# Output projection in products of 512 columns, its rows and weights in another order, and the last job's blocks added one by one

## The reference, cut to what matters

```
merged = sum over four branches of sigmoid(gate_i) * (y_i @ P_i)
x  = x + merged @ W_o                       # W_o: 1024 x 1024
h2 = rmsnorm(x) * norm2_g
x  = x + square(relu(h2 @ W_up)) @ W_down   # W_up: 1024 x 4096, W_down: 4096 x 1024
return x                                    # 512 x 1024
```

## Time and profile before

| | us |
|---|---|
| median of three runs | 1216.63 |
| lowest, highest | 1214.82, 1216.95 |
| the profiled execution's own time | 1213.98 |
| its span in the trace | 1212.2 |
| TensorE busy in the span | 1180.3 |
| DVE, ACT, POOL busy | 504.2, 489.4, 468.8 |

### The profile page before, as it was taken

The page is one execution under the profiler, slowest core; times in us unless marked ns, Lnnn a source line. Parts: engine busy times, 40 slices in busy tenths (PEclk is TensorE's granted clock), DMA queues, the critical chain, the costliest instruction groups (busy, mean ns, idle before and its releaser), DMA issues.

```text
span 1212.2 us, 21083 instructions
## 1 busy us (share of the span) xinstructions
PE 1180.3 (97%) x8974; PEld 973.9 (80%) x8974; DVE 504.2 (42%) x1001; ACT 489.4 (40%) x808; POOL 468.8 (39%) x288
## 2 busy tenths in 40 slices
PE   8999999999999899999999999999899999999998
PEld 7998877887788588667777777789888888888886
DVE  4799435455554544443453676361522000222000
ACT  6455323232223444775726534423543312344220
POOL 3443435325442234323323622433344544344541
PEclk9999999999999999999999999999999999999999
DMA  6222323222221142212522312323122323232330
GB/s 248 88 73 84 115 80 111 69 70 93 98 78 54 35 147 81 64 35 68 193 74 77 104 41 70 138 89 105 53 95 97 122 93 98 71 103 97 112 122 35
DMA packets 35855, 111.49 MB, mean 92 GB/s; under 512 B 4257, under 2 KB 8865, under 8 KB 35250
## 3 DMA queue, kind: packets, MB, share of 16 engines
q1 hardware_dynamic: 30144, 98.59, 24.6%
q10 hardware_dynamic: 5106, 11.43, 2.6%
q0 software_dynamic: 512, 0.13, 0.1%
HBM read 99.43 MB, written 9.04 MB: 89 GB/s over the span
## 4 chain that ended last, share of the span: by engine, by line
PE 81%; DVE 10%; ACT 5%; POOL 2%; issue 2%; DMA 0%; DVEq 0%; ACTq 0%
PE pst L1803 18%; PE pst L1805 17%; PE pst L1804 17%; PE pst L1992 5%; PE pst L1993 5%; PE pst L1994 5%; POOL w_lo L799 1%; PE pst L2314 1%; ACT w_hi L917 1%; PE pst L2306 1%; DVE x_lo L1663 1%; PE pst L2092 1%; PE pst L2039 1%; PE pst L2276 1%; PE pst L2291 1%
## 5 line engine op out<-in xcount | busy, mean ns | idle before, releaser
L799 POOL TENSOR_TENSOR w_lo<-raw,w_hi 128x1024 fp32r<-128x1024 f32 x164 | 402.6, 2461 | 642.4 <-ACT w_hi L917 630.7
L1803 PE MATMUL pst<-h_hi,w_hi 128*128 128x512 f32 (+1 forms) x704 | 255.9, 363 | 1.3 <-DVE h_lo L1369 0.7
L1805 PE MATMUL pst<-h_hi,w_lo 128*128 128x512 f32 (+1 forms) x704 | 243.2, 345 | 0.0
L1804 PE MATMUL pst<-h_lo,w_hi 128*128 128x512 f32 (+1 forms) x704 | 242.9, 345 | 0.0
L917 ACT ACTIVATE w_hi<-raw 128x1024 fp32r<-128x1024 f32 x164 | 171.3, 1051 | 147.7 <-PE pst L1994 114.2
L1803 PEld LDWEIGHTS pst<-h_hi,w_hi 128*128 128x128 f32 x704 | 133.4, 189 | 25.3 <-issue 4.7
L1805 PEld LDWEIGHTS pst<-h_hi,w_lo 128*128 128x128 f32 x704 | 133.3, 189 | 15.9
L1804 PEld LDWEIGHTS pst<-h_lo,w_hi 128*128 128x128 f32 x704 | 133.6, 190 | 15.1 <-issue 2.2
L1803 PE MATMUL pst<-x_hi,w_hi 128*128 128x512 f32 (+1 forms) x272 | 102.7, 377 | 3.8 <-POOL w_lo L799 2.0
L1805 PE MATMUL pst<-x_hi,w_lo 128*128 128x512 f32 (+1 forms) x272 | 102.4, 377 | 0.0
L1804 PE MATMUL pst<-x_lo,w_hi 128*128 128x512 f32 (+1 forms) x272 | 102.4, 376 | 0.0
(11 more groups left out here) (338 smaller groups left out, 2062.9 us busy)
## 6 DMA issues: line engine op xcount, KB each, us to landing
raw<-in_weights SPq DMA_DIRECT2D x164, 512.0 KB, 3.4
xt<-in_x SPq DMA_DIRECT2D x4, 512.0 KB, 5.4
wait_gate<-stage ACTq DMA_DIRECT2D x8, 256.0 KB, 2.7
gate_t<-wait_gate ACTq DMA_DIRECT2D x1, 2048.0 KB, 9.0
x<-in_x ACTq DMA_DIRECT2D x1, 2048.0 KB, 7.8
out<-x SPq DMA_DIRECT2D x8, 256.0 KB, 3.1
cst<-in_consts SPq DMA_DIRECT2D x1, 1524.0 KB, 11.1
wait_ret_g<-stage ACTq DMA_DIRECT2D x4, 256.0 KB, 3.0
```

What stands on the lines that cost most here:

```text
L799: nc.gpsimd.tensor_tensor(w_lo[:, u % W_SLOTS, :], raw[:, u % RAW_SLOTS, :], w_hi[:, u % W_SLOTS, :].bitcast(F32), ALU.subtract).then_inc( ...
L1803: M(out, lh, rh, start=(first and i == 0), stop=False)
L1804: M(out, lh, rl, start=False, stop=False)
L1805: last = M(out, ll, rh, start=False, stop=(final and i == len(terms) - 1))
```

## The change

1. W_o is cut into 2 halves of 512 columns in place of 4 quarters of 256, and a weight unit holds 256 rows by 512 columns of it. A matmul has 512 columns. PHASE_O has 8 jobs (half c, pair of tiles kk).
2. For c = 0, and for kk = 0 of c = 1, a job runs tiles 2kk and 2kk+1 over all four blocks. Each block has a PSUM bank of its own for each half (`wo_bank`). The rest of c = 1 is done block by block in `wo_rows(b)`: 6 tiles by 3 matmuls.
3. DVE adds half 0 in four instructions of 512 columns after job (0, 3), and half 1 of block b in `wo_rows(b)`. On DVE `norm2_low(b - 2)` now stands ahead of the addition of block b.
4. One unit's conversion (`jobs(1)`) stands inside the loop of blocks, and one behind `norm2_low(NB - 1)`, ahead of the up jobs.
5. In the last down job a block's last matmul counts `rows_done`; DVE adds blocks 0 to 2 one by one, and block 3 in two pieces of 256 columns, each with an output DMA of its own.

```diff
-PHASE_O = [("wo", c, b) for c in range(4) for b in range(NB)]
+PHASE_O = [("wo", c, kk) for c in range(2) for kk in range(KD // 2)]
...
     if kind == "wo":
-        return [("w_o", 2 * a), ("w_o", 2 * a + 1)]
+        return [("w_o", b, a)]
...
+            if kind == "wo":
+                return job_out["wo"], 4 * a + max(b - 1, 0)
...
+        def wo_bank(c, blk):
+            if c == 0:
+                return 4 + blk
+            s = job_slot(JOB_NO[("up", 0, 0)])
+            return [2 * s, 2 - 2 * s, 1, 3][blk]
...
-            jobs(len(PHASE_O) - NB - 1)
+            jobs(KD // 2 + 2)
             g("norm2_tables")
-            jobs(1)
             for b in range(NB):
-                jobs(1)
                 if b >= 2:
                     g("norm2_low", b - 2)
+                g("wo_rows", b)
+                if b == NB - 1:
+                    jobs(1)
                 g("norm2", b)
                 if b:
                     g("norm2_turn", b - 1)
...
             g("norm2_low", NB - 1)
+            jobs(1)
             for half in range(2):
...
+            def output(b, c0, c1, added):
+                sp.wait_ge(job_out["down"], added)
+                sp.dma_start(out[0, P * b:P * b + P, c0:c1], x2[:, b, c0:c1]).then_inc(out_done, 16)
+
             for c in range(2):
-                for b in range(NB):
-                    sp.wait_ge(job_out["down"], 8 + 4 * c + b + 1)
-                    sp.dma_start(out[0, P * b:P * b + P, T * c:T * c + T], x2[:, b, T * c:T * c + T])\
-                        .then_inc(out_done, 16)
-            sp.wait_ge(out_done, 16 * 2 * NB)
+                for b in range(NB - c):
+                    output(b, T * c, T * c + T, 8 + 4 * c + b + 1)
+            for i in range(2):
+                output(NB - 1, T + 2 * P * i, T + 2 * P * i + 2 * P, 16 + i)
+            sp.wait_ge(out_done, 16 * (2 * NB + 1))
...
-                act.wait_ge(*all_out("wo", ("wo", 3, b)))
+                act.wait_ge(job_out["wo"], NB + b + 1)
...
                 elif kind == "wo":
-                    dve.wait_ge(x2_in, 16)
-                    dst = x2[:, b, 2 * P * a:2 * P * a + 2 * P]
-                    V.tensor_tensor(dst, pst[:, 2 * s, 0:2 * P], dst, ALU.add).then_inc(job_out[kind], 1)
+                    if (a, b) == (0, KD // 2 - 1):
+                        dve.wait_ge(x2_in, 16)
+                        dve.wait_ge(dense_done, n + 1)
+                        for blk in range(NB):
+                            wo_add(0, blk)
...
+                    if n == len(JOBS) - 1:
+                        for blk in range(NB + 1):
+                            part = slice(T * c, T * c + T)
+                            if blk < NB - 1:
+                                dve.wait_ge(rows_done, NB - 1 + blk + 1)
+                            else:
+                                dve.wait_ge(dense_done, n + 1)
+                            if blk >= NB - 1:
+                                part = slice(T * c + 2 * P * (blk - NB + 1), T * c + 2 * P * (blk - NB + 2))
+                            dst = x2[:, min(blk, NB - 1), part]
+                            src = pst[:, down_bank(c, min(blk, NB - 1)), part.start - T * c:part.stop - T * c]
+                            V.tensor_tensor(dst, src, dst, ALU.add).then_inc(job_out["down"], 1)
...
+            def wo_rows(b):
+                if b < NB - 1:
+                    dve.wait_ge(rows_done, b + 1)
+                else:
+                    dve.wait_ge(dense_done, JOB_NO[PHASE_O[-1]] + 1)
+                wo_add(1, b)
...
+                    if a == 0 or b == 0:
+                        pe.wait_ge(lo_ready, u + 1)
+                        for k in (2 * b, 2 * b + 1):
+                            for blk in range(NB):
+                                if a == blk == 0:
+                                    pe.wait_ge(m_lo, k + 1)
+                                last = wo_part(a, k, blk)
                         last.then_inc(dense_done, 1)
...
+                            if n == len(JOBS) - 1 and j == 1 and blk < NB - 1:
+                                last.then_inc(rows_done, 1)
...
+            def wo_rows(b):
+                for k in range(2, KD):
+                    if b == 0 and k % 2 == 0:
+                        pe.wait_ge(lo_ready, UNIT_NO[("w_o", k // 2, 1)] + 1)
+                    last = wo_part(1, k, b)
+                    if b == NB - 1 and k % 2 == 1:
+                        last.then_inc(dense_done, 1)
+                if b < NB - 1:
+                    last.then_inc(rows_done, 1)
```

More of the change, by code:

```diff
@@ L145 @@
 SPILL_NO = {n: i for i, n in enumerate(n for n, j in enumerate(JOBS) if j[0] in SPILLED)}
-assert all(UNIT_NO[units_of(j)[0]] % 2 == 0 for j in JOBS if j[0] in ("av", "bv", "wo"))
+assert all(UNIT_NO[units_of(j)[0]] % 2 == 0 for j in JOBS if j[0] in ("av", "bv"))
 assert UNIT_NO[("w_in", BV + 2)] % W_SLOTS + 3 <= W_SLOTS
@@ L573, in build @@
         YSW_STEPS = NB
+        rows_done = sem("rows_done")
         br_order = [BRANCH_RW, BRANCH_SB, BRANCH_RET, BRANCH_SW]
@@ L1939, in job @@
                 elif kind == "wo":
-                    job_begin(n)
-                    us = u % W_SLOTS
-                    def wo_part(m, blk, k):
-                        toks = slice(P * blk, P * blk + P)
-                        return product3(pst[:, 2 * job_slot(m), 0:2 * P].rearrange("p (a f) -> p a f", a=2),
-                                        [((x_hi[:, k, toks], x_lo[:, k, toks]),
-                                          (w_hi[:, us:us + 2, P * k:P * k + P], w_lo[:, us:us + 2, P * k:P * k + P]))],
-                                        k == 0, k == KD - 1)
-                    if a == 0 and b < 2:
-                        for k in range(KD - 1):
-                            if b == 0:
-                                pe.wait_ge(m_lo, k + 1)
-                            wo_part(n, b, k)
-                        if b == 1:
-                            pe.wait_ge(m_lo, KD)
-                            wo_part(n - 1, 0, KD - 1).then_inc(dense_done, 1)
-                            wo_part(n, 1, KD - 1).then_inc(dense_done, 1)
-                    else:
-                        for k in range(KD):
-                            last = wo_part(n, b, k)
+                    if a == 0 or b == 0:
[5 more added lines that the diff above has]
+                                last = wo_part(a, k, blk)
                         last.then_inc(dense_done, 1)
@@ L1994, in job, with wo_part @@
                             last = M(o, u_lo[:, f, toks], w_hi[:, us, ws], start=False, stop=(f == FH - 1))
+                            if n == len(JOBS) - 1 and j == 1 and blk < NB - 1:
+                                last.then_inc(rows_done, 1)
                     last.then_inc(dense_done, 1)
+            def wo_part(c, k, blk):
+                u, at_ = UNIT_NO[("w_o", k // 2, c)] % W_SLOTS, T * (k % 2)
+                toks = slice(P * blk, P * blk + P)
+                return product3(pst[:, wo_bank(c, blk), :], [((x_hi[:, k, toks], x_lo[:, k, toks]),
+                                                             (w_hi[:, u, at_:at_ + T], w_lo[:, u, at_:at_ + T]))],
+                                k == 0, k == KD - 1)
+            def wo_rows(b):
[7 more added lines that the diff above has]
+                    last.then_inc(rows_done, 1)
             def sb_rows(h):
@@ L2418, in _ @@
                 ret_out=ret_out, ret_sum=ret_sum, sw_sum=sw_sum, sw_scores=sw_scores,
-                sw_turn=sw_turn, sw_out=sw_out, norm2_turn=norm2_turn, up_early=up_early))
+                sw_turn=sw_turn, sw_out=sw_out, wo_rows=wo_rows, norm2_turn=norm2_turn, up_early=up_early))
 def host_layout(inp):
```

15 lines of the change are left out of this document (9 added, 6 removed).

## The result

| | before | changed |
|---|---|---|
| median | 1215.72 (4 runs, 1214.32 to 1216.95) | 1203.45 (4 runs, 1203.16 to 1203.61) |
| the profiled execution's own time | 1213.98 | 1203.32 |
| its span | 1212.2 | 1201.6 |

The account below looks back on a forecast made before the run. The prediction took TensorE's queue, its waits and the tail behind its last matmul as the bound. A stage gain of 8.1 us and a tail gain of 1.7 made -9.8, giving 1206.8 us, range 1203.8 to 1210.0.

Parts of the forecast that it names:

- Wider products: Output projection: 192 matmuls of 512 columns replace 384 of 256, saving a fixed 0.014 us on each of 192: -2.7 us.
- The first wait: Start of the output projection: the first wo matmul no longer waits for DVE to empty a bank: -0.4 us.
- the short one: Output projection, at 808.81 us: a short wait for an emptied bank goes as well: -0.2 us.
- Weights of wo: Output projection: converted weight units arrive before TensorE wants them, with 4 us of slack: cost 0.
- The norm of each block: Behind the output projection: block 0's turn stops waiting, -1.0; `up_early(0)` waits 0.9 instead of 2.05, -1.2; block 3, +0.1 us.
- The third up unit: Ahead of the third up job: its weights, converted earlier, are ready at 858.7 and wanted at 861.3, removing a wait: -2.1 us.
- The stage as a whole: Output projection through norm: counted forward, the first full up job starts at 861.3 instead of 869.41: -8.1 us.
- The tail: Behind the last matmul: DVE adds blocks as they end and finishes at 1207.8 instead of 1209.49: -1.7 us.
- Total: Whole kernel: -9.8 us, own time 1204.2 for the profiled execution; against the median, 1216.63 - 9.8 = 1206.8.
- a median that lies 2.5 lower in its spread: Low end of the range: the changed kernel's median might lie 2.5 us lower, as the profiled execution does.
- 0.5 for the last DMA: End of the kernel: a smaller last output DMA with an empty queue could gain 0 to 0.5 us; taken as 0.
- the extra conversion on ACT and POOL: Norm stage: ACT's 1.0 us is covered with 0.9 to spare; POOL overlapping block 3's h2n would cost 0.7 at most.

Follow-up runs that it names:

- experiment 7: The changed kernel with each 512-column product of the output projection made of two of 256: 1206.38 us, beside 1204.15 for the changed kernel.
- experiment 2: The kernel before with only the last down job's blocks added as they end and block 3 in two pieces: 1213.05 us, beside 1215.65 unedited.
- experiment 8: The changed kernel, unedited, timed again: 1204.15 us (4 runs), ratio 0.9910 to the kernel before.
- experiment 4: The changed kernel with the third up weight unit converted behind the first up job again, as before: 1207.40 us (5 runs).
- experiment 6: The kernel before, unedited, traced in two more executions: 1215.65 and 1215.26 us.
- experiment 5: The kernel before with the third up weight unit converted early, behind the last wo job: 1211.57 us, beside 1214.92 unedited.
- experiment 11: The changed kernel with its last two down jobs run block by block, plus a gate-job piece between the first two sliding-window score jobs: 1203.57 us.

## Why the sum was right and the range was not

**What held, step by step.** *Wider products*, 2.7: 2.6 by experiment 7, at 0.2266 and 0.1200. *The first wait*, 0.4, and the short one: gone. *Weights of wo*, 0: no wait. *The norm of each block*: the turn of block 0 waits for nothing; ahead of `up_early(0)` 0.63 are left where I had 0.9, because ACT's copies of block 1 led to a low part that ended 846.83 + 1.27, a little sooner than by my steps; block 3 waits for nothing where I had 0.1. POOL's instruction (847.97 to 850.37) ended ahead of block 3's h2n at 850.39, which took 0.75: no collision, by 0.02 us. *The third up unit*: ready at 857.9 (855.51 + 2.40), wanted at 860.76. The stage as a whole: -8.26 for -8.1. *The tail*: -1.85 for -1.7, confirmed alone by experiment 2. Forecast for the profiled execution: own time 1204.2. It was 1203.32; of the 0.9 between them 0.4 lies ahead of all that was changed, 0.2 in the stage, 0.15 in the tail and 0.1 in up and down.

**The step that failed** is the last one, in *Total*: the profiled execution "was 2.65 below the median of the runs shown, which I take as the spread of executions", and all of that was carried over to the changed kernel. In the changed kernel the profiled execution was 0.13 below its median, not 2.65. The spread was no fixed offset that every version of the kernel keeps. The kernel before has two places where TensorE's clock falls to 1.2 GHz for 3.4 us in some executions: the scores, at 1.2 to 1.4 us a fall, and behind the wait for the third up unit, at 1.6 to 1.7. The profiled execution had neither: of 56 others only 10 had a mean clock of 0.999 or more (median 1213.6), and the median of all was 1215.8. Those at 0.996, 23 of them, have a median of 1216.37, 2.8 above 1213.6, and one fall of each kind is 2.8 to 3.1. The change removes the second place with its wait and leaves the first. So of the 12.3 us, about 10.2 are the difference without falls (1213.6 - 1203.45). The other 2.1 are the falls: in part those behind the wait, which can no longer come, and in part luck, since none of the changed kernel's first four executions had the fall in the scores, which it still has in some (10.8 in place of 12.3 by experiment 8).

That the wait brings falls is shown by the traces of experiments 4 and 6, with the half clock right behind it, and by the clocks: a mean of 0.997 or less in 37 of 72 executions with the wait and in 1 of 37 without. The medians of experiments 4 and 5 point the same way, with less certainty.

The lower end of the range did hold "a median that lies 2.5 lower in its spread", 1204.3, and 0.5 for the last DMA. The 0.9 that the sum was short for the profiled execution did not fit into that 0.5, and so the time came out 0.35 below the range. The price of the wait that I took from its row was right as a duration and too low as a cost in the executions with a fall behind it.

One more term of the forecast met its test: the extra conversion on ACT and POOL cost nothing, but by 0.02 us only, so that is luck and not a margin.

**What stays open.** Why a wait of 2 us brings a fall in some executions and not in others is not settled: the same wait stands in each of the four traces of before and in that of experiment 2, and only one of the five has a fall behind it. The wait of 2.05 us ahead of `up_early(0)` is in these five traces and in that of experiment 5, and none has a fall behind it; nor has the wait of 2.3 us in experiment 11. No trace of an execution of before at 0.996 was caught, so its two falls are an estimate from the mean.

## What to carry to other kernels

A wait of TensorE of about 2 us can cost more than its length, since in some executions the clock behind it is at half (1.6 to 1.7 us here): ask of the profiled execution whether it had such a fall or was a lucky one. Look for falls in windows of 1 us, and compare its time and mean clock with those of all runs before a forecast rests on either; the mean also counts the half clock behind the last matmul, which is free. When instructions of two chains share one in-order queue, put the one that waits latest for its input last: what stands behind it pays for its wait. And a product cut in wide pieces saves a fixed part per matmul that is read from the starts, here 13 ns of each.

## What the runs showed of the hardware

- The clock of TensorE fell to 1.2 GHz for some 3.4 us behind 2.1 us of nothing, at 869 us of the kernel before, and also around the end of 3.4 us in which it was never long idle (16 small matmuls, 1.3 us of waiting, 16 small ones, 673.29 to 676.66 us in the changed kernel), in 7 of the 13 traces that have this place. In experiments 4 and 6 the half clock begins less than 1 us behind the first matmul after the wait, so the matmuls that pay are those behind it. The Trainium skill describes the gate in "TensorE: Matmul & The Clock Gate", section "HAM oscillation — how this bites in real kernels", with the cost of the throttled time, half its length, beside that of the wait. The traces agree: the starts are 0.227 and 0.427 us apart for 512 columns, and a fall of 3.4 us behind the wait cost 1.60 and 1.69.
- The output transfers of 1 MB ran at 318 to 420 GB/s without a break. Their queueing costs the end little: spreading the blocks further apart, so that the transfers no longer follow each other without a break, gave only 0.25 us (3.51 for 3.76).
- Behind the last matmul TensorE's granted clock was at half for up to 3.3 us in some traces and not at all in others. It costs nothing and lowers the mean clock of the execution by up to 0.0014.
- The bank of a finished row was read by DVE (0.69 us for 512 columns, at 832.96 and 837.05) while TensorE filled the next at full pace (0.2266), with nothing to be seen on either side: the four additions of half 0 took 2.48 us beside a running TensorE, as the four at the end of the kernel before did beside an idle one.
